# Expert output products from bf16 halves, and gate loads of four blocks, in a two-layer diffusion step on one core

## The chip, the core and the metric

The kernel runs on one core of one Trainium2 chip. The metric is the time of one execution on the device in microseconds (us); the kernel before takes 5205.57 us in the median of three runs (5196.71 to 5222.67). TensorE does the matmuls, VectorE the elementwise work with two tensors, ScalarE the activations and copies, GpSimd issues the indirect gathers, and SyncE issues most of the plain DMA transfers, in the order in which its program has them.

## The reference

The reference is one inference step of a diffusion backbone with two layers over 640 tokens (128 of context and 512 latent ones) of 1024 numbers each: a recurrent mixer in the first layer and attention in the second, and in both a retrieval over 16,384 single-neuron experts. The retrieval is what the change touches:

```python
def _peer(x, w_q, sub_keys, u, v):
    ...
    best, pos = lax.top_k(cand, PEER_TOPK)
    eidx = jnp.take_along_axis(cidx, pos, axis=-1)
    gate = jax.nn.softmax(best, axis=-1)
    ...
    def block(args):
        xb, ib, gb = args
        hb = jax.nn.gelu(jnp.einsum('tkd,td->tk', u[ib], xb), approximate=False)
        return jnp.einsum('tk,tkd->td', gb * hb, v[ib])
```

Each token picks 128 experts (8 heads of 16). Its result is the sum over them of gate times gelu(u·x) times the expert's row of v, all in float32.

## The kernel before

**Two ways to the same sum.** Of the five token tiles of 128, three (`ND = 3`, `TD = 384` tokens) are done densely: the products with all 16,384 experts are made, and a gate that is zero for every expert not picked selects among them. The other two tiles (`NG = 2`) are done by gathering: for each of 128 picks per tile, GpSimd gathers 128 rows of u and v (1 MB for each gather), and VectorE takes a dot product and adds a scaled row. A step of two picks is called a pair; the class `Gather` issues it (line 706) and works it (lines 718 to 733), with room for four pairs on the way.

**The stage that the change touches** is `peer_experts`, the last of each layer's retrieval. It walks 128 tiles n of 128 experts. For tiles below `late` (44 in the first layer, 32 in the second) the hidden products are made here: u is loaded (line 1167), split in a bf16 high half on ScalarE (line 1251) and a low half on VectorE (line 1278), multiplied with the halves of the tokens in three bf16 products (`hidden_products`, line 819), and passed through Gelu on ScalarE (line 1259). For the other tiles the hidden values were made in earlier stages and lie in memory as `hidden`; they are loaded into `est` (line 1183). I call the first kind of tile stretch A, and the second stretch B. In both, VectorE multiplies the values with the gates (line 1294, result `gh`), and TensorE multiplies `gh` with the tile of v (line 1213) and adds up in `psF` over all 128 tiles. These output products are in float32: 6 matmuls of 512 columns for each tile, each of which the trace shows as two.

**The loads.** SyncE issues, for each n in this order: u of tile n+2 (in A), a piece of gates where n+4 begins one (line 1175; a piece is `J = 8` tiles, 1.5 MB, in two buffers), the stored values of tile n+2 (in B), and v of tile n (line 1196). Each waits for its buffer: `stored(n + 2)` for the gating of tile n-1 (three buffers), v for `added` of tile n-3, that is for TensorE's output products of that tile (three buffers). What stands behind a waiting load on this queue waits too.

**The order on VectorE** is written out by hand: the gating of tile n, the low half of u for tile n+3 (in A), then as many pairs as `paired(n)` allows. That table spreads the 81 pairs left in the first layer (85 in the second) so that a tile of A has twice the share of a tile of B: 43 pairs stand in the 44 tiles of A and 38 in the 84 of B (36 in 32, and 49 in 96, in the second layer). In B a tile has one pair or none, mostly in turn, and the last five tiles have none. The order on ScalarE is the Gelu of tile n+1, the high half of u for tile n+3, and the small Gelu of the pairs, which waits for their dot products.

Of the kernel before, what the change touches and what calls it, by code (L numbers as in the profile page):

```python
# [8 lines left out]
P = 128  # L9
D = 1024  # L10
# [1116 lines left out]
def peer_experts(nc, cst, modT, uT, uv, gates, hid, gather, late, h_hi, h_lo, tag):  # L1127


    J, TB = 8, 32  # L1130
    with nc.cleanup_on_exit(), ExitStack() as ctx:
        sb = lambda n, s, d=F32: ctx.enter_context(nc.sbuf_tensor(n + tag, s, d))
        sem = lambda n: nc.alloc_semaphore(n + tag)
# [5 lines left out]
        est = [sb(f"ex_est{s}", [P, TD]) for s in range(3)]  # L1139
        ge = [sb(f"ex_ge{s}", [P, TD]) for s in range(2)]  # L1140
        gh = [sb(f"ex_gh{s}", [P, TD]) for s in range(3)]
        psH = ctx.enter_context(nc.psum_tensor("ex_psH" + tag, [P, 2, BANK], F32))
        psF = ctx.enter_context(nc.psum_tensor("ex_psF" + tag, [P, ND, 2, BANK], F32))
        u_in = [sem(f"ex_u_in{s}") for s in range(3)]
# [2 lines left out]
        e_in = [sem(f"ex_e_in{s}") for s in range(3)]  # L1147
        u_high, u_low = sem("ex_u_high"), sem("ex_u_low")
        made, gelued, gated = sem("ex_made"), sem("ex_gelued"), sem("ex_gated")
        added = sem("ex_added")  # L1150
        copied, turned, summed = sem("ex_copied"), sem("ex_turned"), sem("ex_summed")
        last_sum = sem("ex_last_sum")
# [7 lines left out]
        @block.sync  # L1160
        def _(sp):
            def up(n):
                if n >= late:
                    return
                if n >= 3:
                    sp.wait_ge(u_low, n - 2)
                sp.dma_start(ust[n % 3][:], uT[n]).then_inc(u_in[n % 3], 16)

            def gate(n):
                g = n // J  # L1170
                if n % J or n >= NK:
                    return
                if g >= 2:
                    sp.wait_ge(gated, n - J)
                sp.dma_start(gst[g % 2][:], gates[:, :, n:n + J, :]).then_inc(g_in[g % 2], 16)

            def stored(n):
                if n < late or n >= NK:
                    return
                e = n - late  # L1180
                if e >= 3:
                    sp.wait_ge(gated, n - 2)
                sp.dma_start(est[e % 3][:], hid[n]).then_inc(e_in[e % 3], 16)  # L1183

            for n in range(2):
                up(n)
            gate(0)
            for n in range(2):
                stored(n)
            for n in range(NK):  # L1190
                up(n + 2)
                gate(n + 4)
                stored(n + 2)
                if n >= 3:
                    sp.wait_ge(added, n - 2)
                sp.dma_start(vst[n % 3][:], uv[P * n:P * n + P, D:2 * D]).then_inc(v_in[n % 3], 16)  # L1196

        @block.tensor
        def _(pe):
            def hidden(n):  # L1200
                if n >= late:
                    return
                pe.wait_ge(u_low, n + 1)
                if n >= 2:
                    pe.wait_ge(gelued, n - 1)
                hidden_products(nc, psH[:, n % 2, 0:TD], u_hi[n % 3], u_lo[n % 3], h_hi, h_lo).then_inc(made, 1)

            def output(n):
                pe.wait_ge(v_in[n % 3], 16 * (n // 3) + 16)
                pe.wait_ge(gated, n + 1)  # L1210
                for t in range(ND):
                    for x in range(2):
                        last = nc.tensor.matmul(psF[:, t, x, :], gh[n % 3][:, P * t:P * t + P],  # L1213
                                                vst[n % 3][:, BANK * x:BANK * x + BANK],
                                                start=(n == 0), stop=(n == NK - 1))
                last.then_inc(added, 1)

            hidden(0)
            hidden(1)
            for n in range(NK):  # L1220
                hidden(n + 2)
                output(n)
            for o, t in enumerate(outs):
                if t < ND:
                    pe.wait_ge(copied, t + 1)
                    src, ps = vst[t], psF[:, t]
                else:
                    if t == ND:
                        pe.wait_ge(gelued, late)
                    else:  # L1230
                        pe.wait_ge(summed, o)
                    pe.wait_ge(last_sum, 1)
                    src, ps = gather.acc[t - ND], psH[:]
                ps = ps.rearrange("p x y -> p (x y)")
                for k in range(KD):
                    last = nc.tensor.transpose(ps[:, P * k:P * k + P], src[:, P * k:P * k + P], cst.ident[:])  # L1236
                last.then_inc(turned, 1)
# [5 lines left out]
        @block.scalar  # L1243
        def _(act):
            def take_u(n):
                if n >= late:
                    return
                act.wait_ge(u_in[n % 3], 16 * (n // 3) + 16)
                if n >= 3:
                    act.wait_ge(made, n - 2)  # L1250
                nc.scalar.activation(u_hi[n % 3][:], ust[n % 3][:], ACT.Copy).then_inc(u_high, 1)  # L1251

            def gelu(n):
                if n >= late:
                    return
                act.wait_ge(made, n + 1)
                if n >= 2:
                    act.wait_ge(gated, n - 1)
                nc.scalar.activation(ge[n % 2][:], psH[:, n % 2, 0:TD], ACT.Gelu).then_inc(gelued, 1)

            for n in range(3):
                take_u(n)
            gelu(0)
            for n in range(NK):
                gelu(n + 1)
                take_u(n + 3)
                gather.gelu(act, begun + paired(n))
            act.wait_ge(added, NK)
            for t in range(ND):
                nc.scalar.activation(vst[t][:], psF[:, t].rearrange("p x y -> p (x y)"), ACT.Copy).then_inc(copied, 1)  # L1270

        @block.vector
        def _(dve):
# [8 lines left out]
            for n in range(NK):  # L1282
                if n % J == 0:
                    dve.wait_ge(g_in[n // J % 2], 16 * (n // (2 * J)) + 16)
                if n < late:
                    dve.wait_ge(gelued, n + 1)
                    src = ge[n % 2]
                else:
                    e = n - late
                    dve.wait_ge(e_in[e % 3], 16 * (e // 3) + 16)  # L1290
                    src = est[e % 3]
                if n >= 3:
                    dve.wait_ge(added, n - 2)
                nc.vector.tensor_tensor(gh[n % 3][:].rearrange("p (b t) -> p b t", t=TB),  # L1294
                                        src[:].rearrange("p (b t) -> p b t", t=TB), gst[n // J % 2][:, :, n % J, :],
                                        ALU.mult).then_inc(gated, 1)
                take_u(n + 3)
                while gather.paired < begun + paired(n):
                    gather.pair(dve)
            dve.drain().then_inc(last_sum, 1)  # L1300
# [600 lines left out]
```

## Time and profile before

| what | value |
|---|---|
| median of three runs | 5205.57 us |
| profiled execution, its own time | 5206.45 us |
| its span | 5204.0 us |
| TensorE busy, share of the span | 88% |
| VectorE busy | 62% |
| ScalarE busy | 19% |
| output products (line 1213), busy | 1379.4 us, 3072 matmuls |
| stretch A, first and second layer | 1957 to 2345 us, 4272 to 4558 us |
| stretch B, first and second layer | 2345 to 2858 us, 4558 to 5181 us |

The profiled execution lies 0.9 us above the median, so times from its rows stand for the median run as they are. The four stretches are 1810 us of the 5204; the rest of the program is the same in both kernels. The matmul durations of the trace overlap, so what one matmul costs is read from the distance between two starts, not from its length. In the names, a suffix `_p` stands for both layers' retrieval.

### The profile page before, as it was taken

The numbers are of one execution on the slowest core, as the hardware profiler recorded it, in microseconds if no ns is written. First come the engines' busy times: TensorE is split into PE (matmuls) and PEld (weight loads), VectorE is DVE, ScalarE is ACT, GpSimd is POOL, SyncE is SP. The second block draws the span as 40 slices with busy tenths as digits, with TensorE's granted clock in tenths as the row PEclk, the third lists the DMA queues.
The fourth block names the chain that finished last, engine by engine and source line by source line (L and its number), as shares of the span: only waits on it lengthen the run. The fifth ranks groups of instructions, "written<-read, shape, count | busy, mean of one in ns | idle before, by whom it ended". The sixth has DMA issues, their size and how long they took to land. (4 is left out here: it accounts for less than half of the span.)

```text
span 5204.0 us, 54347 instructions
## 1 busy us (share of the span) xinstructions
PE 4559.8 (88%) x19182; PEld 2677.9 (51%) x19182; DVE 3217.1 (62%) x6385; ACT 989.5 (19%) x1537; POOL 681.0 (13%) x516
## 2 busy tenths in 40 slices
PE   8998894988888999997999877897878989988888
PEld 8776673555554554553434455553444554533333
DVE  0155556368887766774553666268997767765553
ACT  0111100112223431110000245113333431100000
POOL 0000000002221112221110000001221113222110
PEclk9999996998887779998999989998997779999999
DMA  5101100117886769998885100116776669998885
GB/s 201 64 23 44 45 23 24 49 61 285 308 318 239 264 242 362 370 348 316 324 329 209 56 9 1 59 46 226 288 266 243 261 251 358 398 348 324 321 329 186
DMA packets 289233, 1095.11 MB, mean 210 GB/s; under 512 B 28657, under 2 KB 129137, under 8 KB 220017
## 3 DMA queue, kind: packets, MB, share of 16 engines
q0 software_dynamic: 73728, 536.90, 26.6%
q1 hardware_dynamic: 185904, 469.58, 25.6%
q10 hardware_dynamic: 29376, 85.73, 4.3%
q8 instruction: 129, 2.11, 0.2%
q14 instruction: 96, 0.78, 0.0%
HBM read 1002.46 MB, written 89.65 MB: 210 GB/s over the span
## 5 line engine op out<-in xcount | busy, mean ns | idle before, releaser
L1213 PE MATMUL ex_psF_p<-ex_vst_p,ex_gh_p 128*128 128x512 f32 x3072 | 1379.4, 608 | 131.9 <-DMA ex_vst_p<-in_uv 127.9
L706 POOL DMA_INDIRECT room_p<-in_uv,ga_eidx_p x512 | 680.8, 1330 | 4420.4 <-DVEq L733 2343.0
L1213 PEld LDWEIGHTS ex_psF_p<-ex_vst_p,ex_gh_p 128*128 128x128 f32 x3072 | 594.7, 195 | 873.7 <-issue 719.8
L732 DVE SCALAR_TENSOR_TENSOR ga_acc_p<-room_p,ga_gw_p,ga_acc_p 128x1024 f32<-128x1024 f32 x504 | 625.1, 1281 | 22.1 <-issue 2.1
L718 DVE CUSTOM_DVE_ANT_0 room_p<-room_p,hx_p 128x1024 f32<-128x1024 f32 x512 | 605.5, 1220 | 4.8 <-issue 3.8
L819 PE MATMUL eh_psH_sl_p<-h_hi_p,eh_uhi_sl_p 128*128 128x384 bf16 x1056 | 370.9, 351 | 101.5 <-DVE eh_ulo_sl_p L789 101.4
L1294 DVE TENSOR_TENSOR ex_gh_p<-ex_est_p,ex_gst_p 128x384 f32<-128x384 f32 x180 | 100.3, 558 | 533.2 <-PE ex_psF_p L1213 416.2
L819 PE MATMUL eh_psH_sl_p<-h_lo_p,eh_uhi_sl_p 128*128 128x384 bf16 x1056 | 370.1, 350 | 0.0
L819 PE MATMUL eh_psH_sl_p<-h_hi_p,eh_ulo_sl_p 128*128 128x384 bf16 x1056 | 368.5, 349 | 0.0
L312 PE MATMUL rec_psA<-rec_hT,rec_wst 128*128 128x128 f32 (+1 forms) x1024 | 310.2, 450 | 47.5 <-DMA rec_wst<-in_rec_w_in 38.5
L1086 PE MATMUL gt_ps_p<-gt_ohh_p,gt_oh_p 128*128 128x128 bf16 x768 | 316.8, 413 | 34.4 <-DVEq L1072 34.4
L1087 PE MATMUL gt_ps_p<-gt_ohl_p,gt_oh_p 128*128 128x128 bf16 x768 | 317.6, 414 | 0.0
L594 PE MATMUL ps_psA_p<-room_p,ps_wst_p 128*128 128x128 f32 (+1 forms) x1024 | 286.1, 439 | 16.3 <-ACTq L137 16.3
L744 ACT ACTIVATE ga_ge_p<-ga_h_p 128x2 f32<-128x2 f32 x256 | 51.4, 201 | 1306.2 <-DVEq L721 1301.6
L1110 ACT ACTIVATE gt_gs_p<-gt_ps_p 128x1024 f32<-128x1024 f32 x96 | 193.1, 2012 | 169.6 <-PE gt_ps_p L1087 169.6
L819 PE MATMUL ex_psH_p<-h_hi_p,ex_uhi_p 128*128 128x384 bf16 x608 | 200.0, 329 | 26.9 <-DVE ex_ulo_p L1278 26.9
L594 PEld LDWEIGHTS ps_psA_p<-room_p,ps_wst_p 128*128 128x128 f32 x1024 | 154.5, 194 | 127.7 <-issue 125.6
L312 PEld LDWEIGHTS rec_psA<-rec_hT,rec_wst 128*128 128x128 f32 x1024 | 152.1, 199 | 125.7 <-issue 117.0
L819 PEld LDWEIGHTS eh_psH_sl_p<-h_hi_p,eh_uhi_sl_p 128*128 128x128 bf16 x1056 | 115.1, 109 | 194.5 <-DVE eh_ulo_sl_p L789 119.2
L1278 DVE TENSOR_TENSOR ex_ulo_p<-ex_ust_p,ex_uhi_p 128x1024 bf16<-128x1024 f32 x76 | 93.0, 1224 | 183.5 <-ACT ex_uhi_p L1251 183.3
L819 PE MATMUL ex_psH_p<-h_lo_p,ex_uhi_p 128*128 128x384 bf16 x608 | 199.9, 329 | 0.0
L819 PE MATMUL ex_psH_p<-h_hi_p,ex_ulo_p 128*128 128x384 bf16 x608 | 199.7, 329 | 0.0
(232 smaller groups left out, 6177.7 us busy)
## 6 DMA issues: line engine op xcount, KB each, us to landing
ex_vst_p<-in_uv SPq DMA_DIRECT2D x256, 512.0 KB, 7.5
eh_ust_sl_p<-in_uT SPq DMA_DIRECT2D x132, 512.0 KB, 4.1
gates<-gt_gs_p ACTq DMA_DIRECT2D x24, 2048.0 KB, 8.4
ex_gst_p<-gates SPq DMA_DIRECT2D x32, 1536.0 KB, 17.4
ex_ust_p<-in_uT SPq DMA_DIRECT2D x76, 512.0 KB, 8.8
ex_est_p<-hidden SPq DMA_DIRECT2D x180, 192.0 KB, 7.8
hidden<-eh_ge_sl_p ACTq DMA_DIRECT2D x132, 192.0 KB, 4.3
ada_wst<-in_ada_w SPq DMA_DIRECT2D x48, 512.0 KB, 3.3
```

The costliest lines, as they stand in the source:

```text
L312: last = nc.tensor.matmul(out, lhs, rhs, start=(k == 0), stop=(k == KD - 1))
L594: last = nc.tensor.matmul(psA[s % 2][:, col], wst[s][:, k, :], hT[:, k, tok], start=(k == 0), stop=(k == KD - 1))
L706: self.nc.gpsimd.indirect_dma_start(self.slot[s % self.RING], None, self.uv, bass.IndirectOffsetOnAxis(self.eidx[:, s:s + 1], 0)).then_inc ...
L718: nc.vector.tensor_tensor_reduce(out=row, in0=row, in1=self.hx[:, s // W, :], scale=1.0, scalar=0.0, op0=ALU.mult, op1=ALU.add, accum_out= ...
L732: nc.vector.scalar_tensor_tensor(acc[:], row, self.gw[:, s:s + 1], acc[:], op0=ALU.mult, op1=ALU.add)
L819: last = nc.tensor.matmul(ps, a[:, k, :], b[:, k, :], start=(m == 0), stop=(m == len(prods) - 1))
L1086: nc.tensor.matmul(o, oh2[n % 3][:, :, x], ohh[n % 3][:, :, x], start=True, stop=False)
L1087: last = nc.tensor.matmul(o, oh2[n % 3][:, :, x], ohl[n % 3][:, :, x], start=False, stop=True)
L1110: nc.scalar.activation(gs[b % 2][:, :, TI * q:TI * q + TI].rearrange("p j t -> p t j"), ps[n % 3][:], ACT.Copy).then_inc(ev, 1)
L1213: last = nc.tensor.matmul(psF[:, t, x, :], gh[n % 3][:, P * t:P * t + P], vst[n % 3][:, BANK * x:BANK * x + BANK], start=(n == 0), stop=(n ...
L1278: nc.vector.tensor_tensor(u_lo[n % 3][:], ust[n % 3][:], u_hi[n % 3][:], ALU.subtract).then_inc(u_low, 1)
L1294: nc.vector.tensor_tensor(gh[n % 3][:].rearrange("p (b t) -> p b t", t=TB), src[:].rearrange("p (b t) -> p b t", t=TB), gst[n // J % 2][:, ...
```

## The change

The output product of a tile is made from bf16 halves. ScalarE copies v into `v_hi` (bf16), VectorE subtracts that from v into `v_lo`; ScalarE copies `gh` into `g_hi` and VectorE makes `g_lo`. TensorE then makes three bf16 products (high times high, high times low, low times high), 18 matmuls of 512 columns for each tile, in place of 6 in float32. The new buffers are threefold. To make room for them a piece of gates has 4 tiles rather than 8 (`J = 4`): twice as many loads, each half as large. The load of v waits for the low half of tile n-3 in place of its output products. The core of the diff:

```diff
-    J, TB = 8, 32
+    J, TB = 4, 32
...
                 if n >= 3:
-                    sp.wait_ge(added, n - 2)
+                    sp.wait_ge(v_low, n - 2)
                 sp.dma_start(vst[n % 3][:], uv[P * n:P * n + P, D:2 * D]).then_inc(v_in[n % 3], 16)
...
             def output(n):
-                pe.wait_ge(v_in[n % 3], 16 * (n // 3) + 16)
-                pe.wait_ge(gated, n + 1)
+                pe.wait_ge(v_low, n + 1)
+                pe.wait_ge(g_low, n + 1)
+                prods = ((g_hi, v_hi), (g_hi, v_lo), (g_lo, v_hi))
                 for t in range(ND):
...
+            def take_v(n):
+                act.wait_ge(v_in[n % 3], 16 * (n // 3) + 16)
+                if n >= 3:
+                    act.wait_ge(added, n - 2)
+                nc.scalar.activation(v_hi[n % 3][:], vst[n % 3][:], ACT.Copy).then_inc(v_high, 1)
+
+            def take_g(n):
+                act.wait_ge(gated, n + 1)
+                if n >= 3:
+                    act.wait_ge(added, n - 2)
+                nc.scalar.activation(g_hi[n % 3][:], gh[n % 3][:], ACT.Copy).then_inc(g_high, 1)
...
             for n in range(NK):
+                take_v(n)
                 gelu(n + 1)
                 take_u(n + 3)
+                take_g(n)
                 gather.gelu(act, begun + paired(n))
...
                 if n >= 3:
-                    dve.wait_ge(added, n - 2)
+                    dve.wait_ge(g_high, n - 2)
                 nc.vector.tensor_tensor(gh[n % 3][:].rearrange("p (b t) -> p b t", t=TB),
...
+                dve.wait_ge(v_high, n + 1)
+                if n >= 3:
+                    dve.wait_ge(added, n - 2)
+                nc.vector.tensor_tensor(v_lo[n % 3][:], vst[n % 3][:], v_hi[n % 3][:], ALU.subtract).then_inc(v_low, 1)
                 take_u(n + 3)
+                dve.wait_ge(g_high, n + 1)
+                nc.vector.tensor_tensor(g_lo[n % 3][:], gh[n % 3][:], g_hi[n % 3][:], ALU.subtract).then_inc(g_low, 1)
```

On VectorE in stretch B, in the kernel before, a tile is its gating (`ex_gh`), and then the operations of a pair where one is due (dot products on `room`, then `ga_gw` and two additions to `ga_acc`):

```order
L1294 TENSOR_TENSOR ex_gh_p<-ex_est_p,ex_gst_p 128x384 x2
L718 ISA room_p,ga_h_p<-room_p,hx_p 128x1024
L718 ISA ga_h_p 128x1
L718 ISA room_p,ga_h_p<-room_p,hx_p 128x1024
L718 ISA ga_h_p 128x1
L725 TENSOR_TENSOR ga_gw_p<-ga_ge_p,ga_gsel_p 128x2
L732 SCALAR_TENSOR_TENSOR ga_acc_p<-room_p,ga_gw_p,ga_acc_p 128x1024 x2
```

In the changed kernel, the same place:

```order
L1315 TENSOR_TENSOR ex_gh_p<-ex_est_p,ex_gst_p 128x384
L1321 TENSOR_TENSOR ex_vlo_p<-ex_vst_p,ex_vhi_p 128x1024
L1324 TENSOR_TENSOR ex_glo_p<-ex_gh_p,ex_ghi_p 128x384
L1315 TENSOR_TENSOR ex_gh_p<-ex_est_p,ex_gst_p 128x384
L1321 TENSOR_TENSOR ex_vlo_p<-ex_vst_p,ex_vhi_p 128x1024
L1324 TENSOR_TENSOR ex_glo_p<-ex_gh_p,ex_ghi_p 128x384
L718 ISA room_p,ga_h_p<-room_p,hx_p 128x1024
L718 ISA ga_h_p 128x1
L718 ISA room_p,ga_h_p<-room_p,hx_p 128x1024
L718 ISA ga_h_p 128x1
L725 TENSOR_TENSOR ga_gw_p<-ga_ge_p,ga_gsel_p 128x2
L732 SCALAR_TENSOR_TENSOR ga_acc_p<-room_p,ga_gw_p,ga_acc_p 128x1024 x2
```

The low half of v (`ex_vlo`) and that of the gated values (`ex_glo`) now stand between the gating of a tile and its pair, so the next gating and the next pair stand behind them.

On SyncE's queue in stretch B, in the kernel before, around a load of gates (`ex_gst`, 12 blocks of 256 numbers for each partition), with the stored values (`ex_est`) and v (`ex_vst`):

```order
L1183 DMA ex_est_p<-hidden 128x384
L1196 DMA ex_vst_p<-in_uv 128x1024
L1175 DMA ex_gst_p<-gates 128x12x256
L1183 DMA ex_est_p<-hidden 128x384
L1196 DMA ex_vst_p<-in_uv 128x1024
L1183 DMA ex_est_p<-hidden 128x384
L1196 DMA ex_vst_p<-in_uv 128x1024
```

In the changed kernel, around such a load:

```order
L1188 DMA ex_est_p<-hidden 128x384
L1201 DMA ex_vst_p<-in_uv 128x1024
L1180 DMA ex_gst_p<-gates 128x12x128
L1188 DMA ex_est_p<-hidden 128x384
L1201 DMA ex_vst_p<-in_uv 128x1024
L1188 DMA ex_est_p<-hidden 128x384
L1201 DMA ex_vst_p<-in_uv 128x1024
```

The order of the three kinds of load is kept, a load of gates has half the width (12 blocks of 128 numbers) and stands at every fourth tile rather than every eighth. The load of v of a tile still stands behind that of the stored values of two tiles later.

## Rows read from the trace of the kernel before

**Rows 1.** Busy time by stretch: A and B of the first layer, then second

```profile
core 0: us, PE busy (x) PEld busy (x) DVE busy (x) ACT busy (x) POOL busy (x), PEclk, DMA share, GB/s
1957.00:2345.00 388.00, 388.00 (x1557) 197.80 (x1556) 284.47 (x385) 69.83 (x128) 106.63 (x84) 1.00 0.95 360
2345.00:2858.00 513.00, 463.15 (x1034) 201.55 (x1033) 236.42 (x352) 7.74 (x38) 75.31 (x71) 0.95 0.81 296
4272.00:4558.00 286.00, 270.82 (x1082) 137.42 (x1083) 211.29 (x285) 51.79 (x95) 82.41 (x62) 0.97 0.95 372
4558.00:5181.00 623.00, 545.91 (x1224) 237.34 (x1223) 316.79 (x469) 11.25 (x54) 116.71 (x100) 0.93 0.83 308
```

**Rows 2.** Timeline of TensorE, stretch A: start, length, operation, count

```profile
4557.49 5.31 PE L1213 MATMUL ex_psF_p<-ex_vst_p,ex_gh_p 128*128 128x512 f32 x12
4562.64 0.33 PE L819 MATMUL ex_psH_p<-h_hi_p,ex_uhi_p 128*128 128x384 bf16 x1
...
4566.54 1.02 PE L1213 MATMUL ex_psF_p<-ex_vst_p,ex_gh_p 128*128 128x512 f32 x2
```

**Rows 3.** Timeline of VectorE, stretch B: a tile with a pair

```profile
2545.86 0.56 DVE L1294 TENSOR_TENSOR ex_gh_p<-ex_est_p,ex_gst_p 128x384 f32<-128x384 f32 x1 [3.86 <-PE ex_psF_p L1213]
2546.34 1.22 DVE L718 CUSTOM_DVE_ANT_0 room_p<-room_p,hx_p 128x1024 f32<-128x1024 f32 x1
...
2551.74 0.56 DVE L1294 TENSOR_TENSOR ex_gh_p<-ex_est_p,ex_gst_p 128x384 f32<-128x384 f32 x1 [0.19 <-issue]
```

**Rows 4.** Groups by line, stretch A: count, busy, mean ns, idle before

```profile
L1278 DVE TENSOR_TENSOR ex_ulo_p<-ex_ust_p,ex_uhi_p 128x1024 bf16<-128x1024 f32 x41 | 50.2, 1224 | 81.8 <-ACT ex_uhi_p L1251 81.8
L1251 ACT ACTIVATE ex_uhi_p<-ex_ust_p 128x1024 bf16<-128x1024 f32 x41 | 43.0, 1049 | 18.7 <-DMA ex_ust_p<-in_uT 18.6
```

**Rows 5.** Waits of SyncE's queue, stretch B, first layer: total, times, longest

```profile
SPq L1196 <- PE ex_psF_p L1213: 329.8, 78, 10.4
SPq L1183 <- DVE ex_gh_p L1294: 72.4, 73, 7.8
```

**Rows 6.** Timeline of SyncE's queue, stretch B, around a load of gates

```profile
2546.15 0.72 SPq L1175 DMA_DIRECT2D ex_gst_p<-gates  x1
2546.91 5.59 SPq L1183 DMA_DIRECT2D ex_est_p<-hidden  x1
2552.55 0.61 SPq L1196 DMA_DIRECT2D ex_vst_p<-in_uv  x1
```

**Rows 7.** Timeline of GpSimd beside Rows 3: the first gather after that pair

```profile
2551.85 1.26 POOL L706 DMA_INDIRECT room_p<-in_uv,ga_eidx_p  x1 [7.79 <-DVEq L733]
```

**Rows 8.** Landing of one block of v, no gather under way

```profile
DMA to landing us min/median/max: 3.5/3.5/3.5
```

**Rows 9.** Landing of all 84 blocks of v, stretch B, first layer

```profile
DMA to landing us min/median/max: 3.4/6.2/23.6
```

**Rows 10.** Landing of 97 blocks of v, stretch B, second layer

```profile
DMA to landing us min/median/max: 3.5/8.0/22.8
```

**Rows 11.** Landing of the block of v in Rows 6, behind the gates

```profile
DMA to landing us min/median/max: 13.2/13.2/13.2
```

**Rows 12.** TensorE's weight loads after a wait, stretch B

```profile
2518.03 0.30 PEld L1213 LDWEIGHTS ex_psF_p<-ex_vst_p,ex_gh_p 128*128 128x128 f32 x2 [4.84 <-DMA ex_vst_p<-in_uv]
...
2519.27 0.34 PEld L1213 LDWEIGHTS ex_psF_p<-ex_vst_p,ex_gh_p 128*128 128x128 f32 x1 [0.51 <-issue]
2520.12 0.34 PEld L1213 LDWEIGHTS ex_psF_p<-ex_vst_p,ex_gh_p 128*128 128x128 f32 x1 [0.52 <-issue]
...
2522.41 0.19 PEld L1213 LDWEIGHTS ex_psF_p<-ex_vst_p,ex_gh_p 128*128 128x128 f32 x1 [0.24 <-issue]
2522.84 0.19 PEld L1213 LDWEIGHTS ex_psF_p<-ex_vst_p,ex_gh_p 128*128 128x128 f32 x1 [0.24 <-issue]
```

**Rows 13.** Waits of VectorE and TensorE, stretch B, first layer

```profile
DVE ex_gh_p L1294 <- PE ex_psF_p L1213: 205.6, 47, 8.0
PE ex_psF_p L1213 <- DMA ex_vst_p<-in_uv: 49.8, 10, 13.8
```

More of the change, by code:

```diff
@@ L1141, in peer_experts @@
         gh = [sb(f"ex_gh{s}", [P, TD]) for s in range(3)]
+        v_hi = [sb(f"ex_vhi{s}", [P, D], BF16) for s in range(3)]
+        v_lo = [sb(f"ex_vlo{s}", [P, D], BF16) for s in range(3)]
+        g_hi = [sb(f"ex_ghi{s}", [P, TD], BF16) for s in range(3)]
+        g_lo = [sb(f"ex_glo{s}", [P, TD], BF16) for s in range(3)]
         psH = ctx.enter_context(nc.psum_tensor("ex_psH" + tag, [P, 2, BANK], F32))
@@ L1149, in peer_experts @@
         made, gelued, gated = sem("ex_made"), sem("ex_gelued"), sem("ex_gated")
+        v_high, v_low, g_high, g_low = sem("ex_v_high"), sem("ex_v_low"), sem("ex_g_high"), sem("ex_g_low")
         added = sem("ex_added")
@@ L1208, in output @@
             def output(n):
-                pe.wait_ge(v_in[n % 3], 16 * (n // 3) + 16)
-                pe.wait_ge(gated, n + 1)
+                pe.wait_ge(v_low, n + 1)
+                pe.wait_ge(g_low, n + 1)
+                prods = ((g_hi, v_hi), (g_hi, v_lo), (g_lo, v_hi))
                 for t in range(ND):
[L1212 to L1215, printed above, removed]
+                    for i, (a, b) in enumerate(prods):
+                        for x in range(2):
+                            last = nc.tensor.matmul(psF[:, t, x, :], a[n % 3][:, P * t:P * t + P],
+                                                    b[n % 3][:, BANK * x:BANK * x + BANK],
+                                                    start=(n == 0 and i == 0), stop=(n == NK - 1 and i == 2))
                 last.then_inc(added, 1)
```

## The prediction, as it was put on record

> **What bounds the kernel now.** I read the busy time by stretch first, since the change touches only the four stretches of `peer_experts`. In A of the first layer TensorE is busy for all 388 us at a granted clock of 1.00, which is 2.4 GHz, while VectorE is busy for 284 [rows 1]. So A is TensorE's, at 9.05 us for a tile: the 12 float32 matmuls of a tile take 5.15 us from first start to the next operation, and the 24 hidden products 3.90 [rows 2]. In B TensorE is busy for 463 of 513 us and for 546 of 623 [rows 1]; what it waits for in the first layer is v, 10 times and 49.8 us in all [rows 13]. A tile of B takes 6.1 and 6.5 us, of which the products are 5.15. VectorE waits there for TensorE, 205.6 us in all [rows 13], so it runs some three tiles ahead of it. Transfers are the second limit: their share is 0.95 in A and 0.81 to 0.83 in B [rows 1].
>
> The waits of SyncE's queue say how v gets its lead: its load waits nearly always for output products (78 times), and the load of stored values ahead of it waits 73 times for a gating, 72.4 us in all [rows 5]. Because VectorE is ahead, that gating is mostly done early, and v is asked for two tiles before TensorE needs it.
>
> **The change part by part.** *Output products.* 18 bf16 matmuls of 512 columns replace 12 float32 ones. The hidden products cost 3.90 / 24 = 0.163 us for 384 columns [rows 2], so 512 cost 0.217 and a tile 3.9 us rather than 5.15. That takes 1.25 us for each of 256 tiles off TensorE, 320 us in all, if nothing else comes to bound.
>
> *VectorE.* The low half of v has the shape and types of the low half of u, 1.22 us [rows 4], 1.2 from start to start. The low half of the gated values has the size of the gating; from one gating to the operation behind it are 0.5 us [rows 3]. A pair takes 5.4 us, from its first dot product to the next gating [rows 3]. So a tile's own work is 0.5 + 1.2 + 0.5 = 2.2 us in B, and 3.4 in A with the low half of u. ScalarE gets a copy of 1.05 us [rows 4] and one of about half of that; it has the room.
>
> *The load of v becomes a wait of VectorE, and this is the term that decides.* In the old order only TensorE waited for v. Now VectorE itself needs v of tile n, cast by ScalarE, before it may go on to the low half of `gh`, the pair and the next gating. And in B the queue issues v of tile n behind the stored values of tile n+2, which wait for the gating of tile n-1. That wait was there before [rows 5] and cost little because VectorE was ahead; now the gating of tile n-1 is one tile ahead of the need. Where tile n-1 has no pair, there are only 2.2 us of VectorE work between that gating and the point where v is wanted. Where it has one, the pair covers the load. Pairs stand on every other tile, so every second load is bare. Counted from the end of the gating of a tile without a pair to the same point two tiles later:
>
> - the queue issues stored values and then v: 0.4 us;
> - v lands: 8.0 us;
> - ScalarE's high half with the handing over: 1.05 + 0.2;
> - low half of v, low half of `gh`, pair, next gating: 1.2 + 0.5 + 5.4 + 0.56.
>
> That is 17.3 us for two tiles. The landing is bounded by 3.5 us where no gather is under way [rows 8], and by 13.2 where the block stands behind a load of gates [rows 11]; the medians are 6.2 and 8.0 [rows 9, 10]. I take 8.0: the bare load goes out right behind a pair, and at the end of a pair GpSimd issues two gathers, the first 0.1 us after the gating starts [rows 3, 7], so the bare load always meets 2 MB of gathers. It is the upper median for that reason.
>
> The table of pairs gives, in B of the first layer, 37 such couples, and 10 further tiles, which I put at the 5.2 us that they cost TensorE before: 37 x 17.3 + 52 = 692 us, against 513: +179. In the second layer there are 41 couples, 8 tiles with a pair behind a tile with a pair (half a cycle, 8.7) and 6 others: 709 + 70 + 31 = 810, against 623: +187.
>
> *Gates in pieces of four.* A piece is loaded into the buffer that the four tiles before last used, so at every fourth tile it waits for the gating of tile n-1, in A too, and v of tile n stands behind it. Before, at every eighth tile, that buffer had long been free. How long does a piece delay v? The old one was issued at 2546.15, the transfers behind it stuck until 2552.55, and v landed 13.2 us after that [rows 6, 11]: 19.6 us after the piece, against 8.4 without one, 11.2 more for 1.5 MB. Half of it by proportion is 5.6; the bytes alone, 0.77 MB at the 372 GB/s of A [rows 1], are 2.1. I take the middle, 3.9, and keep both for the range. In B 22 pieces fall on a bare load (11 in each layer); the others are covered by the pair. 22 x 3.9 = +86.
>
> *Stretch A.* VectorE's work is 44 x 3.4 + 43 x 5.4 = 382 us in the first layer, against 388 now (-6), and 32 x 3.4 + 36 x 5.4 = 303 against 286 in the second (+17). So A passes from TensorE to VectorE at about the old time, and TensorE's gain of 1.25 us for each tile is worth nothing. On top come the pieces: from the gating of tile n-1 VectorE has 8.8 us of work until it wants v (1.2 + 1.2 + 0.5 + 5.4 + 0.5), and v comes after 0.4 + 8.0 + 3.9 + 1.25 = 13.6. The stall is 4.75 us, at 10 tiles in the first layer and 7 in the second: +81.
>
> **The sum.** 366 + 86 + 11 + 81 = +544 us. The profiled execution took 5206.45 us, 0.9 above the median of three, so the forecast is 5750 us.
>
> **The rivals.**
>
> *v comes in time, faster.* Were v asked for early enough, A would stand at +11 and B would be bound by what is left: VectorE's 84 x 2.2 + 38 x 5.4 = 390 us and 476 in the second layer, or by the transfers, 513 us at 296 GB/s and 623 at 308 [rows 1], which at 372 GB/s take 408 and 516. That is 924 for 1136: 5206 + 11 - 212 = 5005 us. Against it: a bare load would have to land 0.6 us after its issue (2.2 less 1.65 for issue and cast), and the shortest landing is 3.4 [rows 9]. 3%.
>
> *The landing is short, about no change.* With two gathers only, and no queue of older loads, v might land near its floor. At 3.5 us [rows 8] a cycle is 12.8 us: 526 and 617 us in B (+13 and -6), +11 in A, no stall from the pieces in A, 46 in B with 2.1 us each: 5270 us. It decides itself where the landing of bare loads falls under about 5 us. For it speaks that the transfers are less crowded when tiles take longer; against it, that the gathers always go out just ahead. 9%.
> On the landing, the Trainium skill (DMA: Bandwidth & Descriptors, "Anatomy of one DMA") puts one transfer at about 2 us plus its bytes at 436 GB/s, which would be 3.2 us for 0.52 MB, an estimate from that page. The block without a gather beside it agrees, with 3.5 [rows 8]; the medians of 6.2 and 8.0 [rows 9, 10] don't, and by the page's figure alone the time would be near this rival's.
>
> *The landing waits for both gathers.* If v gets little of the engines until the gathers are through, it lands after 11 us or more: 78 cycles x 3 = +234, and 51 more in A: 6035 us. 7%.
>
> *TensorE becomes the bound at the lower clock.* After a wait of 4.8 us for v the weight loads follow one another at 0.85 us instead of 0.43, until 2522.4 [rows 12]: 1.2 GHz in place of 2.4. With longer waits it may start each tile like that. A tile of B then costs up to 7.8 us, which is under the 8.7 of the cycle, so the sum of B stays. In A a tile would cost up to 15.6 us, 76 x 6.6 = +500 less the 92 counted there: 6160 us. A's waits are short (TensorE works 7.8 of 8.8 us), and I give it 1%.
> The Trainium skill (TensorE: Matmul & The Clock Gate, "HAM oscillation") states the same rule, that waits for transfers between groups of matmuls put the engine back to the lower clock; it speaks against the first rival as well, since a B at 7.8 us for a tile is slower than today's 6.1. The row agrees with it for that one wait [rows 12].
>
> **Chances and range.** My forecast, with its ends, holds 80%. The low end takes a landing of 6.2 (78 cycles x -1.8 = -140, and 17 x -1.8 = -31) and pieces at 2.1 (-71): 5508. The high end takes 10 us and 5.6: +156 + 34 + 66 = 6006. Both ends together are unlikely; the range is 5490 to 5960. A measurement can tell about 0.5% (26 us) from no change. Faster by more: 3%; within: 3%, a part of the second rival; slower: 94%.
>
> **What would show it.** In the profile after: VectorE's low half of v waits in B for ScalarE's copy, ScalarE's copy for the load of v, several us each, at every second tile and most where the tile before has no pair; TensorE is busy for about half of B and waits for VectorE's low half of `gh`; SyncE's stored values wait for the gating nearly always. A tile of B takes 8 to 9 us, one of A 9 to 10.5, and A's stalls come at every fourth tile. The products of a tile take 3.9 us at full clock. Wrong would be the whole of it if the low half of v hardly waits: then v is early, the queue is not what I take it for, and the time falls towards 5005. If the waits are there and B still takes 6 us for a tile, the landing was too high; if TensorE, not VectorE, is busy throughout A, it is the clock.

## The result and the profile after

The changed kernel takes 5726.47 us in the median of four runs (5724.18 to 5743.52), against 5201.14 for the kernel before: 1.101 times as long, with a 95% interval from 1.097 to 1.105. The prediction was 5750. The profiled execution of the changed kernel is the longest of the four, with a span of 5741.8 us, 538 above that of before.

Of these 538 us, some 526 lie in the four stretches. By the timelines, from the first gating of a stretch to that of the next (or to the last output product):

| stretch | before | after | added | forecast |
|---|---|---|---|---|
| A, first layer | 385 | 439 | +54 | -6 + 48 = +42 |
| B, first layer | 510 | 702 | +192 | 179 + 43 = +222 |
| A, second layer | 294 | 346 | +52 | 17 + 33 = +50 |
| B, second layer | 599 | 827 | +228 | 187 + 43 = +230 |

Busy time by stretch in the changed kernel, to be read beside [rows 1] (the columns are those of the first line):

```profile
core 0: us, PE busy (x) PEld busy (x) DVE busy (x) ACT busy (x) POOL busy (x), PEclk, DMA share, GB/s
1971.00:2410.00 439.00, 356.08 (x1787) 180.12 (x1817) 355.68 (x475) 129.62 (x215) 123.32 (x84) 0.92 0.83 318
2410.00:3113.00 703.00, 416.06 (x1491) 162.08 (x1521) 367.72 (x516) 132.82 (x206) 89.37 (x70) 0.82 0.59 213
4545.00:4890.00 345.00, 262.73 (x1285) 131.41 (x1307) 280.93 (x378) 94.37 (x160) 102.32 (x70) 0.89 0.84 317
4890.00:5717.00 827.00, 470.62 (x1700) 183.49 (x1733) 448.74 (x629) 152.23 (x240) 115.31 (x92) 0.82 0.62 223
```

In B neither TensorE (416 of 703 us, and at a granted clock of 0.82), nor VectorE (368), nor the transfers (a share of 0.59 where it was 0.81) is full any longer: a stage in which everything waits. Who waits for whom in B of the first layer (total, times, longest), first ScalarE, VectorE and TensorE, then SyncE's queue:

```profile
ACT ex_vhi_p L1272 <- DMA ex_vst_p<-in_uv: 345.1, 56, 12.9
DVE ex_vlo_p L1321 <- ACT ex_vhi_p L1272: 310.4, 43, 12.5
PE ex_psF_p L1220 <- DVE ex_glo_p L1324: 284.3, 75, 10.6
```

```profile
SPq L1188 <- DVE ex_gh_p L1315: 396.0, 56, 18.5
SPq L1180 <- DVE ex_gh_p L1315: 149.1, 19, 14.5
```

It is one chain. ScalarE waits for the load of v, VectorE for ScalarE's high half, 43 times and 7.2 us in the mean, and TensorE for VectorE's last low half. On the queue the load of the stored values waits 396 us for gatings, where it was 72.4 [rows 5], and the wait of v for output products (329.8 us, [rows 5]) is gone. In the other direction nearly nothing is left: until the sums are copied out at the end of B in the first layer, VectorE never waits for TensorE there, and ScalarE does once, for 1.3 us.

One couple of tiles in B, from the timelines of GpSimd, SyncE's queue, VectorE and ScalarE (start, length, engine, line, operation, and the idle time before with what ended it):

```profile
2589.20 1.29 POOL L706 DMA_INDIRECT room_p<-in_uv,ga_eidx_p  x1 [14.34 <-DVEq L733]
2589.70 0.33 SPq L1188 DMA_DIRECT2D ex_est_p<-hidden  x1
2590.07 0.43 SPq L1201 DMA_DIRECT2D ex_vst_p<-in_uv  x1
2591.20 0.55 DVE L1315 TENSOR_TENSOR ex_gh_p<-ex_est_p,ex_gst_p 128x384 f32<-128x384 f32 x1
...
2597.30 1.06 ACT L1272 ACTIVATE ex_vhi_p<-ex_vst_p 128x1024 bf16<-128x1024 f32 x1 [7.07 <-DMA ex_vst_p<-in_uv]
...
2598.39 1.23 DVE L1321 TENSOR_TENSOR ex_vlo_p<-ex_vst_p,ex_vhi_p 128x1024 bf16<-128x1024 f32 x1 [6.64 <-ACT ex_vhi_p L1272]
...
2605.40 0.56 DVE L1315 TENSOR_TENSOR ex_gh_p<-ex_est_p,ex_gst_p 128x384 f32<-128x384 f32 x1 [0.19 <-issue]
```

The gating of a tile without a pair ends at 2589.67, and the queue issues the stored values (2589.70) and v (2590.07) at once. A gather went out half a us earlier. VectorE reaches the next gating at 2591.20 and then has nothing that it may do: v lands at 2597.3, ScalarE casts it, and the low half of v starts at 2598.39 after 6.64 us idle. Then come the low half of `gh`, the pair, and the next gating at 2605.40, so the couple takes 16.3 us from one gating's end (2589.67) to the other's (2605.96). The forecast cycle was 17.3. The landing of all blocks of v in this stretch, against [rows 9]:

```profile
DMA to landing us min/median/max: 3.4/8.0/12.5
```

A bare load behind a piece of gates, on SyncE's queue and then on VectorE:

```profile
2804.39 0.52 SPq L1180 DMA_DIRECT2D ex_gst_p<-gates  x1
2804.96 0.96 SPq L1188 DMA_DIRECT2D ex_est_p<-hidden  x1
2805.96 1.26 SPq L1201 DMA_DIRECT2D ex_vst_p<-in_uv  x1
```

```profile
2805.88 0.55 DVE L1315 TENSOR_TENSOR ex_gh_p<-ex_est_p,ex_gst_p 128x384 f32<-128x384 f32 x1
...
2818.88 1.23 DVE L1321 TENSOR_TENSOR ex_vlo_p<-ex_vst_p,ex_vhi_p 128x1024 bf16<-128x1024 f32 x1 [12.45 <-ACT ex_vhi_p L1272]
...
2826.25 0.56 DVE L1315 TENSOR_TENSOR ex_gh_p<-ex_est_p,ex_gst_p 128x384 f32<-128x384 f32 x1 [0.19 <-issue]
```

The gating that begins at 2803.80 frees the queue, and out go the piece, the stored values and v, in that order. VectorE gates the next tile at 2805.88 and is then idle for 12.45 us. From the end of the one gating (2804.36) to that two tiles later (2826.81) are 22.5 us, 6.2 more than in the couple above. This is one of the longest; the mean of all couples is in the section on the prediction.

In A, around such a tile on VectorE:

```profile
2133.45 0.56 DVE L1315 TENSOR_TENSOR ex_gh_p<-ex_ge_p,ex_gst_p 128x384 f32<-128x384 f32 x1 [0.22 <-issue]
2139.76 1.23 DVE L1321 TENSOR_TENSOR ex_vlo_p<-ex_vst_p,ex_vhi_p 128x1024 bf16<-128x1024 f32 x1 [5.75 <-ACT ex_vhi_p L1272]
2143.23 1.22 DVE L1299 TENSOR_TENSOR ex_ulo_p<-ex_ust_p,ex_uhi_p 128x1024 bf16<-128x1024 f32 x1 [2.24 <-ACT ex_uhi_p L1258]
```

There are two waits here, one for v (5.75 us) and one for u (2.24 us): u of tile n+3 stands behind the same piece as v of tile n. Over the whole of A in the first layer (from 1965 us on; total, times, longest):

```profile
DVE ex_vlo_p L1321 <- ACT ex_vhi_p L1272: 50.9, 11, 6.0
DVE ex_ulo_p L1299 <- ACT ex_uhi_p L1258: 17.8, 9, 2.9
```

### The profile page after: what moved, and what is told of

It reads as the page before. It is cut to its first block and busy times, and to the rows that moved or that the text cites. A ratio compares the mean times of both kernels' runs of the same rounds, so it can differ in the third digit from the quotient of the medians.

```text
span 5741.8 us, 59104 instructions
## 1 busy us (share of the span) xinstructions
PE 4412.5 (77%) x20597; PEld 2569.7 (45%) x20718; DVE 3626.3 (63%) x6897; ACT 1362.8 (24%) x2049; POOL 730.0 (13%) x516
## 5 line engine op out<-in xcount | busy, mean ns | idle before, releaser
L706 POOL DMA_INDIRECT room_p<-in_uv,ga_eidx_p x512 | 729.8, 1425 | 4909.5 <-DVEq L733 2819.9
L1220 PE MATMUL ex_psF_p<-ex_vhi_p,ex_ghi_p 128*128 128x512 bf16 x1495 | 530.4, 439 | 802.1 <-DVE ex_glo_p L1324 800.6
L1321 DVE TENSOR_TENSOR ex_vlo_p<-ex_vst_p,ex_vhi_p 128x1024 bf16<-128x1024 f32 x256 | 312.6, 1221 | 754.3 <-ACT ex_vhi_p L1272 754.2
L1220 PEld LDWEIGHTS ex_psF_p<-ex_vhi_p,ex_ghi_p 128*128 128x128 bf16 x1536 | 150.6, 107 | 1058.1 <-DVE ex_vlo_p L1321 728.8
L1220 PE MATMUL ex_psF_p<-ex_vlo_p,ex_ghi_p 128*128 128x512 bf16 x1496 | 521.4, 432 | 3.1 <-issue 1.3
L1220 PE MATMUL ex_psF_p<-ex_vhi_p,ex_glo_p 128*128 128x512 bf16 x1496 | 511.9, 425 | 3.3 <-issue 1.3
L1272 ACT ACTIVATE ex_vhi_p<-ex_vst_p 128x1024 bf16<-128x1024 f32 x256 | 268.6, 1049 | 882.8 <-DMA ex_vst_p<-in_uv 881.2
L594 PE MATMUL ps_psA_p<-room_p,ps_wst_p 128*128 128x128 f32 (+1 forms) x1024 | 287.9, 441 | 16.3 <-ACTq L137 16.3
L1220 PEld LDWEIGHTS ex_psF_p<-ex_vlo_p,ex_ghi_p 128*128 128x128 bf16 x1536 | 167.9, 109 | 243.8 <-issue 109.7
L1220 PEld LDWEIGHTS ex_psF_p<-ex_vhi_p,ex_glo_p 128*128 128x128 bf16 x1536 | 165.6, 108 | 233.3 <-issue 90.3
```

What stands on the lines that cost most here:

```text
L594: last = nc.tensor.matmul(psA[s % 2][:, col], wst[s][:, k, :], hT[:, k, tok], start=(k == 0), stop=(k == KD - 1))
L706: self.nc.gpsimd.indirect_dma_start(self.slot[s % self.RING], None, self.uv, bass.IndirectOffsetOnAxis(self.eidx[:, s:s + 1], 0)).then_inc ...
L1220: last = nc.tensor.matmul(psF[:, t, x, :], a[n % 3][:, P * t:P * t + P], b[n % 3][:, BANK * x:BANK * x + BANK], start=(n == 0 and i == 0), ...
L1272: nc.scalar.activation(v_hi[n % 3][:], vst[n % 3][:], ACT.Copy).then_inc(v_high, 1)
L1321: nc.vector.tensor_tensor(v_lo[n % 3][:], vst[n % 3][:], v_hi[n % 3][:], ALU.subtract).then_inc(v_low, 1)
```

## The experiments

All kernels were run beside the kernel before. "The first edit" and "the second" are the names of the two changes to SyncE's queue of which the fastest version is made.

**The load of v ahead of the waiting loads.**

```diff
+            value(0)
             for n in range(NK):
                 up(n + 2)
+                value(n + 1)
                 gate(n + 4)
                 stored(n + 2)
-                if n >= 3:
-                    sp.wait_ge(v_low, n - 2)
-                sp.dma_start(vst[n % 3][:], uv[P * n:P * n + P, D:2 * D]).then_inc(v_in[n % 3], 16)
```

(`value(n)` holds the three lines that went.)

> The changed kernel with one edit on SyncE's queue: v of tile n+1 is issued ahead of the gates and the stored values of iteration n, as soon as its buffer is free, rather than v of tile n behind them. All work is kept. Theory (the load of v stands behind the wait for a gating, and VectorE waits for it): the waits of VectorE for v go. Stretch A falls to VectorE's work, about 385 us in the first layer and 310 in the second (445 and 350 in the changed kernel); stretch B to what VectorE and the transfers allow, about 420 and 520 us (698 and 828). About 5010 us in all, between 4960 and 5100. Rival (VectorE's 512 added subtractions, some 430 us of work, are the cost): the work is the same, so within 1% of the changed kernel's 5726. Rival (TensorE at the lower clock sets the pace): over 5500.

Measured: 5119.65 us, 0.983 of before (0.980 to 0.987). With the same work on every engine 607 us are gone, and the kernel is faster than that before. That settles it against the added work. Busy time by stretch (columns as above), A and B of the first layer:

```profile
1976.00:2391.00 415.00, 354.89 (x1789) 180.16 (x1819) 355.17 (x476) 129.71 (x217) 123.56 (x85) 0.94 0.90 341
2391.00:2823.00 432.00, 344.81 (x1484) 147.91 (x1516) 365.90 (x515) 130.67 (x205) 88.88 (x70) 0.97 0.92 344
```

B is 432 us, and 518 in the second layer, as expected. VectorE's wait for v is nearly gone from it; 400 of the 432 us, from 2400 to 2800, have this row left of the 310.4 us above:

```profile
DVE ex_vlo_p L1327 <- ACT ex_vhi_p L1278: 27.0, 13, 2.9
```

The granted clock rises to 0.97 with the same matmuls, so the low clock followed the waits. A is not as expected: 415, and 330 in the second layer, where 385 and 310 were expected, and that puts the whole 20 us above the stated range. Among the waits of A in the first layer (total, times, longest) there is now:

```profile
DVE ex_ulo_p L1305 <- ACT ex_uhi_p L1264: 42.1, 11, 6.1
```

It is the low half of u: with v out of the way, u behind the waiting piece is what comes late. My expectation had charged A's stalls to v alone.

**The pair ahead of the low halves.**

```diff
                 ...then_inc(gated, 1)
+                while gather.paired < begun + paired(n):
+                    gather.pair(dve)
                 dve.wait_ge(v_high, n + 1)
...
                 nc.vector.tensor_tensor(g_lo[n % 3][:], gh[n % 3][:], g_hi[n % 3][:], ALU.subtract).then_inc(g_low, 1)
-                while gather.paired < begun + paired(n):
-                    gather.pair(dve)
```

> The changed kernel with one edit on VectorE: the pair of a tile stands ahead of its low half of v, rather than behind both low halves. The queue of the loads and all work are kept. Theory: each load of v gets a pair or two tiles of work as cover; two tiles of B take 2.2 us of work plus 9 us from a gating to the high half of v, about 11.2 us rather than the 16.2 measured, and A's stalls go, since the cover there becomes 14 us. About 5350 us, between 5280 and 5450. Rival (the work): within 1% of 5726. Rival (each transfer of v is simply too slow, whatever the order): within 2% of 5726.

Measured: 5311.58 us (1.021 of before). The queue's order is what it was; only the work that covers the load has moved. Busy time of A and B in the first layer:

```profile
1963.00:2346.00 383.00, 340.01 (x1773) 174.35 (x1803) 354.35 (x475) 129.99 (x216) 131.81 (x85) 0.99 0.96 366
2346.00:2893.00 547.00, 380.46 (x1501) 157.47 (x1533) 366.01 (x516) 130.23 (x205) 98.83 (x70) 0.88 0.75 274
```

A stands at 383 and 303 us, where the prediction counted 382 and 303 of work for VectorE: with a cover of 14 us its waits for v are gone there, and 8 us of waits for u are left in the first layer. B keeps part of its waits, 547 and 648 us; in the first layer VectorE still waits 161 us for ScalarE's high half of v, rather than 310.

**The same work without a wait for v.**

```diff
-                dve.wait_ge(v_high, n + 1)
-                if n >= 3:
-                    dve.wait_ge(added, n - 2)
-                nc.vector.tensor_tensor(v_lo[n % 3][:], vst[n % 3][:], v_hi[n % 3][:], ALU.subtract).then_inc(v_low, 1)
+                nc.vector.tensor_tensor(v_lo[n % 3][:], gather.hx[:, 0, :],
+                                        h_hi[:].rearrange("p k t -> p (k t)")[:, 0:D], ALU.subtract)
```

(Not shown: the load of v and TensorE wait for the high half of v in place of the low one, and `take_v(n)` stands last in ScalarE's loop.)

> The changed kernel with VectorE's subtraction for v made on data that always lies ready (tokens and their high halves), of the same size and types, so that VectorE does the same work and never waits for v; TensorE multiplies with the high half of v twice, so the result leaves out the low half of v. ScalarE's copy of v stands last in its iteration, so that it holds up no other copy. Theory: VectorE no longer waits, TensorE alone does, three tiles behind; about 5030 us, between 4970 and 5130. Rival (VectorE's added work is the cost): within 1% of 5726.

Measured: 5275.56 us (1.014 of before). The work stays and 451 us go, so the rival falls, but 246 us more were expected to go. One row among the waits in B of the first layer (2400 to 2800 us; total, times, longest) tells a good part of it:

```profile
DVE ex_glo_p L1322 <- ACT ex_ghi_p L1278: 82.6, 24, 10.1
```

VectorE's low half of `gh` waits for ScalarE's high half of it, and ScalarE works in order: its copy of v, which waits for the load, stands ahead of the next copy of `gh`. The wait for v had been taken off VectorE and came back to it through ScalarE. TensorE's own wait for v, which had been expected, is there too (108 us in the same 400). In A the piece still holds up u: A takes 432 us, and VectorE waits 58.7 us for the high half of u. The run bounds the cost of the work from above and is no clean measure of it.

**A piece of gates two tiles ahead.**

```diff
                 up(n + 2)
-                gate(n + 4)
+                gate(n + 2)
                 stored(n + 2)
```

> The changed kernel with one number changed: a piece of gates is issued two tiles ahead of its first tile rather than four, so that its buffer is free by then and the load of v behind it doesn't stand behind a wait. Theory: in A the stalls of every fourth tile go (445 and 350 us become about 390 and 310), in B nothing changes, since the stored values' wait holds v there in any case; about 5630 us, between 5600 and 5670. Rival (pieces of half the width cost by their transfers, 512-byte runs, not by their wait): within 0.5% of 5726.

Measured: 5524.93 us (1.062 of before), 202 us less, where about 95 were expected. Busy time of A and B in the first layer:

```profile
1975.00:2350.00 375.00, 343.45 (x1787) 176.07 (x1817) 353.94 (x476) 129.37 (x216) 133.60 (x84) 0.99 0.98 374
2350.00:3002.00 652.00, 413.78 (x1481) 161.04 (x1513) 367.81 (x515) 131.10 (x204) 89.39 (x70) 0.85 0.65 229
```

A did what was expected and a little more: 375 us, and 298 in the second layer, and of its stalls, those of u and of v, under 4 us are left in each layer. But B fell as well, from 703 and 827 to 652 and 772. There the piece had gone out at the same moment as the bare load of v and ahead of it. Now it needs no wait of its own, as SyncE's timeline in B shows:

```profile
2611.47 0.33 SPq L1188 DMA_DIRECT2D ex_est_p<-hidden  x1
2611.84 0.43 SPq L1201 DMA_DIRECT2D ex_vst_p<-in_uv  x1
2612.32 0.52 SPq L1180 DMA_DIRECT2D ex_gst_p<-gates  x1
2613.55 4.71 SPq L1188 DMA_DIRECT2D ex_est_p<-hidden  x1
```

The stored values and the bare v go out at 2611.47 and 2611.84, the piece only behind them, and it delays the next v, which a pair covers. Where the next v is the bare one, the piece is mostly some 14 us ahead of it. Bare loads land after some 7.5 us in the mean here, as those without a piece do in the changed kernel.

**Both edits together.** The first edit and the second, nothing else.

> The changed kernel with both edits on SyncE's queue: v of tile n+1 ahead of the gates and the stored values, and a piece of gates two tiles ahead rather than four. What is left in the first edit's stretch A are stalls at every fourth tile, where VectorE's low half of u waits: u of tile n+3 still stands behind the waiting piece. Theory: the second edit takes these, so A stands at VectorE's work as with that edit alone (375 and 298 us) and B as with the first edit alone (432 and 518): about 5050 us, between 5030 and 5085. Rival (the stalls of A are the crowded transfers, not the wait): within 0.5% of 5120.

Measured: 5036.60 us, 0.968 of the kernel before (0.966 to 0.970). This version beats both kernels. Busy time of the four stretches in the profiled execution, which is the fastest of five (5021 us):

```profile
1966.00:2343.00 377.00, 341.28 (x1780) 174.57 (x1810) 354.20 (x476) 128.73 (x215) 133.93 (x85) 1.00 0.99 375
2343.00:2761.00 418.00, 346.90 (x1486) 149.26 (x1518) 365.50 (x515) 130.94 (x205) 89.46 (x70) 0.96 0.96 355
4191.00:4491.00 300.00, 255.75 (x1284) 129.03 (x1306) 280.68 (x379) 94.43 (x161) 108.49 (x70) 0.94 0.97 370
4491.00:4996.00 505.00, 401.84 (x1700) 170.68 (x1734) 445.99 (x629) 151.40 (x239) 117.50 (x92) 0.95 0.97 363
```

A is VectorE's (354 us busy of 377, with 14 us of waits) and B is shared by VectorE (366 of 418) and the transfers, whose share is 0.96 or more in all four stretches.

**The first edit in the kernel before.** The same diff, with `added` in place of `v_low`.

> The kernel before, float32 products and pieces of eight, with the first edit alone: v of tile n+1 is issued ahead of the gates and the stored values, as soon as its buffer is free. Theory: TensorE's waits for v in B (50 us in the first layer, 76 in the second) go, A stays with TensorE and the transfers; about 5080 us, between 5040 and 5130, so that most of what the changed kernel gains with that edit comes from the queue and the bf16 products are worth under 1.5%. Rival (v is no limit of the kernel before): within 0.5% of 5205.

Measured: 5222.91 us, 1.003 of before (1.001 to 1.005): no gain, and far outside the expected range. TensorE's waits for v in B didn't go, they fell to 38 us in each layer. B fell from 510 and 599 to 486 and 547 us, and A rose from 385 and 294 to 421 and 332. The waits that grew, in B and in A (41.7 us and 81.8 us in the kernel before):

```profile
DVE ex_gh_p L1300 <- DMA ex_est_p<-hidden: 194.3, 43, 15.7
```

```profile
DVE ex_ulo_p L1284 <- ACT ex_uhi_p L1257: 126.0, 23, 14.7
```

In the float32 kernel the buffer of v is freed late, by TensorE. A load of v one tile further ahead waits for that (353 us in all in B of the first layer, 361 in A), and now the stored values (194 us of waits) and u stand behind it. The same order of loads that is right when VectorE frees v is a trap when TensorE does.

**No gathers in the second layer's last stage.** The first layer is untouched; in the second, GpSimd issues none and VectorE doesn't wait for them.

```diff
-            gather.issue(pool, gather.PAIRS)
+            gather.issue(pool, gather.fetched)
...
+        if tag == "_p1":
+            gather.fetched = gather.issued
```

> The changed kernel with the gathers of the second layer's last stage left out (VectorE does the pairs on the rows that lie in the buffers, so the result leaves those rows out); the first layer is untouched. It measures what the gathers beside a bare load of v cost. Theory: v lands in about 3.5 us rather than 7.3, so a couple of tiles in the second B takes 12.4 us rather than 16.2, and the pieces cost less: B of the second layer falls from 827 us to about 630, A from 346 to about 320, the first layer stays; about 5505 us, between 5460 and 5570. Rival (v's own load takes its time, whatever runs beside it): within 1% of 5726.

Measured: 5510.68 us (1.059 of before). The landing of v in that B:

```profile
DMA to landing us min/median/max: 3.2/4.1/7.9
```

It falls from a median of 8.0 us to 4.1, and the stretch from 827 to 645 us. A of that layer falls from 346 to 300, where 320 was expected; the first layer stays, at 433 and 708. The bare loads alone, without a piece ahead of them, land after 3.5 us in the median rather than 7.5, and a couple takes 12.7 us rather than 16.9 in the mean. About half of the landing of a bare load is the gathers beside it. The stretch still stands 127 us above the 518 that the first edit gives with all gathers: a short landing alone doesn't make up for the order.

**Pieces of four in the kernel before.**

```diff
-    J, TB = 8, 32
+    J, TB = 4, 32
```

> The kernel before with pieces of four blocks of gates in place of eight, and nothing else of the change. Theory: the piece waits for a gating here as well, but VectorE gates tiles ahead of TensorE, which alone waits for v, so nearly nothing is late: within 1% of 5205. Rival (pieces of four cost by themselves, by their wait or their short runs): 100 us or more slower.

Measured: 5191.52 us, 0.999 of before (0.997 to 1.000). The verdict is the expected one, the reason was not: it isn't that nothing is late. A rose to 411 and 342 us and B fell to 453 and 558. In A, VectorE's wait for the high half of u (81.8 us before), and in B TensorE's wait for v (49.8 us, [rows 13]):

```profile
DVE ex_ulo_p L1278 <- ACT ex_uhi_p L1251: 111.9, 15, 13.5
```

```profile
PE ex_psF_p L1213 <- DMA ex_vst_p<-in_uv: 14.6, 5, 10.7
```

In B of the first layer, v behind a piece lands after 8.1 us in the median, where it was 13.3 behind the larger one. In A the piece waits 177 us in all for a gating, where it waited for nothing (0.3 us), and u stands behind it. The next run tests the second; that the first is what shortens B is not tested by itself.

**Pieces of four, two tiles ahead, in float32.** The second edit on the kernel of the last run.

> The kernel before, float32 products, with pieces of four blocks of gates, each issued two tiles ahead rather than four. It asks how much of the fastest version so far (5037 us, bf16 halves, v ahead, pieces two tiles ahead) is the queue and how much the products. Theory: with pieces of four alone, A lost 74 us, since u stood behind the waiting piece, and B won 98, since a piece holds the queue half as long; two tiles ahead the piece waits for nothing, so A returns to 385 and 294 us and B stays near 453 and 558: about 5110 us, between 5080 and 5145. Then the bf16 products are worth about 1.5% more, in stretch B alone. Rival (with the queue put right float32 goes as fast): at or under 5050. Rival (B's gain and A's loss are one thing, work that only moves from one stretch to the next): within 0.5% of 5192.

Measured: 5111.88 us, 0.983 of before (0.981 to 0.985). Busy time of A and B in the first layer:

```profile
1964.00:2350.00 386.00, 386.00 (x1538) 196.40 (x1536) 286.55 (x388) 68.39 (x127) 99.04 (x85) 1.00 0.96 360
2350.00:2803.00 453.00, 442.94 (x1028) 195.09 (x1027) 232.81 (x347) 7.58 (x38) 77.29 (x70) 0.99 0.91 332
```

A is back (386, and 289 in the second layer), B stays (453 and 557). So the wait of the piece was A's loss, and B's gain is not work that moved. The queue alone, with half pieces asked for later, is worth 1.7% in float32, and the bf16 products with their own order of loads another 1.5% (5036.60). Whether another order would take float32 further was not tried.

## Why the prediction was right

**What decides.** That VectorE, and through it everything else, would wait for a load that stands behind a wait for the gating one tile before: the couple of tiles shows it instruction by instruction, the first edit removes it with all work kept, and moving the pair removes most of it with the queue kept. The rival of work is excluded by the first edit. That of the clock is excluded by the waits: TensorE waits 284 us for VectorE in B of the first layer alone, and VectorE never waits for TensorE in any of the four stretches. The first rival's time, 5005 us for a v that comes early, was a fair estimate too: both edits on the queue together reach 5037. The signs that it named are there: a tile of B takes 8.4 and 8.6 us, one of A 10.0 and 10.8 (the last a little over the 10.5), and TensorE is busy for 59% of B in the first layer.

**The sizes.** In absolute times the forecast of the four stretches was 430, 735, 336 and 853 us, and the trace has 439, 702, 346 and 827: 40 us less in all. The increments agree better, since the prediction took the old times from round windows [rows 1]. Its second B begins at 4558 us, 25 us before the first gating of that stretch, so that 623 stood for 599, and 286 for 294 in A. So the close agreement in the second layer's B (+228 for +230) is luck.

The terms can be counted over all 78 couples in the timelines. The 59 with no piece ahead of the bare load take 16.7 us in the mean rather than 17.3, since their v lands after 7.6 us rather than 8.0. The 19 with a piece take 21.4, 4.7 us more; 3.9 had been taken, for 22 of them. So the couples were put some 46 us too high, and the pieces in B came out as forecast, 89 us for 86; the 6.2 us of the example above are not typical. The 24 other tiles of B took 137 us for 153.

**Stretch A.** The total came out within 10 us in each layer, by two errors that cancel. VectorE's work was put a little too high: the second edit alone leaves next to no waits, and A stands at 375 and 298 us, where 382 and 303 were counted. The stalls at every fourth tile came as forecast, 51 and 41 us of waits for v where 48 and 33 were counted. But the wait for u, put at nothing, adds some 15 and 9 us from the first gating on, and the first edit alone, which takes only v out of the piece's way, leaves A at 415 and 330. The piece delays all that stands behind it.

**TensorE's clock.** The prediction let it cost nothing in B. In a tile after a wait of 4.76 us, two bf16 matmuls at a time (start, length, count):

```profile
2600.23 0.64 PE L1220 MATMUL ex_psF_p<-ex_vhi_p,ex_ghi_p 128*128 128x512 bf16 x2 [4.76 <-DVE ex_glo_p L1324]
2600.66 1.06 PE L1220 MATMUL ex_psF_p<-ex_vlo_p,ex_ghi_p 128*128 128x512 bf16 x2
2601.51 1.06 PE L1220 MATMUL ex_psF_p<-ex_vhi_p,ex_glo_p 128*128 128x512 bf16 x2
...
2604.07 0.60 PE L1220 MATMUL ex_psF_p<-ex_vhi_p,ex_glo_p 128*128 128x512 bf16 x2
2604.50 0.59 PE L1220 MATMUL ex_psF_p<-ex_vhi_p,ex_ghi_p 128*128 128x512 bf16 x2
```

The first two matmuls take 0.43 us to the next start, then each two take 0.85 us, and 0.43 again from 2604.07 on: the lower level of the clock is 1.2 GHz, the higher 2.4. The tile takes 5.7 us instead of 3.9, still far under the cycle. By the Trainium skill (TensorE: Matmul & The Clock Gate, "HAM oscillation") waits for transfers between groups of matmuls put the engine back to the lower clock. This trace agrees, with a granted clock of 0.82 in B against 0.95 before; here TensorE waits for the low halves, and they wait for the load of v. The lower clock followed from the waits and did not set the time: with the order of loads mended it is 0.97 in the same stretch, and in the changed kernel nothing waits for TensorE there but ScalarE, once, for 1.3 us, and at the end, to copy out the sums.

**The short landing.** The rival at 5270 us needed a bare v within about 5 us. Without gathers it would have had it: 3.5 us in the median for the bare loads without a piece ahead, and a couple of 12.7 us for the rival's 12.8. B of the second layer took 645 us; the rival gave it 617 (its own cycle makes 607 of it) and counted 23 for the pieces besides. Beside the gathers it never had the chance. The fit of the Trainium skill that the prediction set beside this rival (DMA: Bandwidth & Descriptors, "Anatomy of one DMA") is given there for transfers that GpSimd issues, while SyncE issues v, so the 3.2 us worked out from it are an estimate for a near case.

## What to carry to other kernels

Before a consumer moves from one engine to another, ask how far ahead each of them runs: a load that was early for an engine three tiles behind can be bare for one that is only a tile behind its own request. On a queue that issues in order, put first what has a free buffer, and a load that must wait as late as its use allows; the right order follows from who frees each buffer, so the same edit gained 607 us here and nothing in the kernel before. And when a wait is taken off an engine, look along the in-order engines that feed it, since there it may come back.

## What was not expected of the hardware

In the couple shown, the stored values that go out half a us after a gather landed after 2.3 us, and the bare v behind them after 7.2, at 2597.3: 0.4 us after that gather, which took 7.6 us, and before the second one, issued at 2590.79. So here a load of 0.5 MB lands as late as 1 MB that another queue had begun 0.9 us earlier. In B of the second layer a bare load without a piece ahead takes 3.5 us in the median without gathers, against 7.5 beside two of them for each couple: the gathers cost a load about its own time once more.
